# Two transformer blocks on one core: another order and other queues for the first transfers, and products of ones ahead of the work

## What is computed

```python
h = rmsnorm(x, norm_attn[l])
proj = h @ w_in[l]
qa, ka, va, qb, kb, vb = jnp.split(proj, splits, axis=-1)
...
yb = diff_attention(qb, kb, vb, lam)
yb = (rmsnorm(yb, subln[l], SUBLN_EPS) * (1.0 - lam_init)).astype(x.dtype).reshape(B, S, B_WIDTH)
x = x + jnp.concatenate([ya, yb], axis=-1) @ w_out[l]
h = rmsnorm(x, norm_ffn[l])
x = x + (jax.nn.silu(h @ w_gate[l]) * (h @ w_up[l])) @ w_down[l]
```

## Time and profile before

| | us |
|---|---|
| median of 3 runs | 2584.1 |
| lowest and highest | 2583.82, 2584.75 |
| the profiled execution | 2584.64 |
| its span | 2582.8 |
| TensorE busy in it | 2562.9 (99%) |
| VectorE, ScalarE, GpSimd busy | 1453.2, 1224.1, 104.4 |

### The profile page before, as it was taken

One profiled execution on the slowest core, in us unless ns is written; L12 is line 12 of the kernel. 1 busy time (PEld: TensorE's weight loads), 2 busy tenths in 40 slices (PEclk: granted clock), 3 DMA queues, 4 the chain that ended last, 5 costly groups with the idle time before them and its releaser, 6 DMA issues.

```text
span 2582.8 us, 40276 instructions
## 1 busy us (share of the span) xinstructions
PE 2562.9 (99%) x14246; PEld 2280.2 (88%) x14246; DVE 1453.2 (56%) x1743; ACT 1224.1 (47%) x1677; POOL 104.4 (4%) x171
## 2 busy tenths in 40 slices
PE   8999999999999999999999999999999999999999
PEld 8999988888888888888899888788999899998997
DVE  5555555555555555555455545465576646765674
ACT  5665545444344434455455544544454434543443
POOL 1111100000000000000000000100000000000000
PEclk9999999999999999999999999999999999999999
DMA  7555556665665566666555655555555555555554
GB/s 214 155 159 162 168 183 186 189 188 192 193 191 187 189 194 191 191 196 188 166 168 170 187 170 172 163 171 185 176 181 184 195 189 185 181 188 194 173 191 165
DMA packets 328631, 469.37 MB, mean 182 GB/s; under 512 B 21911, under 2 KB 137810, under 8 KB 328402
## 3 DMA queue, kind: packets, MB, share of 16 engines
q1 hardware_dynamic: 328530, 468.04, 58.1%
HBM read 465.87 MB, written 2.10 MB: 181 GB/s over the span
## 4 chain that ended last, share of the span: by engine, by line
PE 84%; issue 14%; POOL 1%; SPq 0%; DMA 0%; DVE 0%; ACT 0%; POOLq 0%; DVEq 0%; ACTq 0%
PE ps L429 20%; PE ps L431 20%; PE ps L430 20%; PE ps L443 7%; PE ps L442 7%; PE ps L441 7%; PE ps L498 1%; PE ps L645 1%; PE ps L676 0%; PE ps L549 0%; POOL head_rstd L1844 0%; PE ps L480 0%; PE ps L486 0%; PE ps L568 0%; SPq L328 0%
## 5 line engine op out<-in xcount | busy, mean ns | idle before, releaser
L1276 DVE TENSOR_TENSOR w_lo<-raw,w_hi 128x1024 fp32r<-128x1024 f32 (+1 forms) x928 | 1095.3, 1185 | 1080.3 <-ACT w_hi L879 1079.0
L879 ACT ACTIVATE w_hi<-raw 128x1024 fp32r<-128x1024 f32 (+1 forms) x928 | 947.7, 1025 | 1151.0 <-PE ps L431 961.6
L429 PE MATMUL ps<-w_hi,xT_hi 128*128 128x512 f32 (+1 forms) x2400 | 906.8, 378 | 2.9 <-DVE w_lo L1276 2.8
L431 PE MATMUL ps<-w_hi,xT_lo 128*128 128x512 f32 (+1 forms) x2400 | 893.6, 372 | 0.0
L430 PE MATMUL ps<-w_lo,xT_hi 128*128 128x512 f32 (+1 forms) x2400 | 892.9, 372 | 0.0
L429 PEld LDWEIGHTS ps<-w_hi,xT_hi 128*128 128x128 f32 x2400 | 451.5, 188 | 69.4 <-issue 6.6
L431 PEld LDWEIGHTS ps<-w_hi,xT_lo 128*128 128x128 f32 x2400 | 451.1, 188 | 64.3
L430 PEld LDWEIGHTS ps<-w_lo,xT_hi 128*128 128x128 f32 x2400 | 451.7, 188 | 62.4
L441 PE MATMUL ps<-yT_hi,w_hi 128*128 128x256 f32 x1408 | 398.6, 283 | 0.0
L443 PE MATMUL ps<-yT_hi,w_lo 128*128 128x256 f32 x1408 | 398.5, 283 | 0.0
L442 PE MATMUL ps<-yT_lo,w_hi 128*128 128x256 f32 x1408 | 398.5, 283 | 0.0
(11 more groups left out here) (191 smaller groups left out, 994.4 us busy)
## 6 DMA issues: line engine op xcount, KB each, us to landing
raw<-in_w_up SPq DMA_DIRECT2D x264, 512.0 KB, 3.6
raw<-in_w_down SPq DMA_DIRECT2D x176, 512.0 KB, 4.4
raw<-in_w_in SPq DMA_DIRECT2D x112, 512.0 KB, 3.7
raw<-in_w_in SPq DMA_DIRECT2D x256, 192.0 KB, 2.6
raw<-in_w_gate SPq DMA_DIRECT2D x88, 512.0 KB, 3.5
raw<-in_w_out SPq DMA_DIRECT2D x60, 512.0 KB, 4.1
raw<-in_w_in SPq DMA_DIRECT2D x64, 384.0 KB, 3.3
raw<-in_w_proj_m SPq DMA_DIRECT2D x16, 512.0 KB, 3.5
```

The source lines that it names most:

```text
L429: pe.matmul(o, hi[:, q], w_hi[n % NS][:, k, 0:width], start=first, stop=False)
L431: mm = pe.matmul(o, lo[:, q], w_hi[n % NS][:, k, 0:width], start=False, stop=last)
L879: nc.scalar.activation(w_hi[n % NS][:, :, 0:width], raw[n % NS][:, :, 0:width], ACT.Copy).then_inc(hi_ready, 1)
L1276: v.tensor_tensor(w_lo[n % NS][:, :, 0:width], raw[n % NS][:, :, 0:width], f32(w_hi[n % NS][:, :, 0:width]), ALU.subtract).then_inc(lo_rea ...
```

## The change

- SP asks for x first, and in eight pieces of 256 columns (256 KB), one ahead of unit 0 and one behind each of units 0 to 6. Piece j counts `x_landed[j % 4]`; pieces 4 to 7 are asked for only when piece j - 4 has landed. TensorE waits for piece 0 and 1 each ahead of its pair, and for each later pair's own.
- The identity and then the gain rows are asked for by ScalarE, as the first thing it does.
- The other 21 small transfers are asked for by GpSimd, between its memsets and `factor(1, rstd)`: fourteen (`small`) when `lo_ready` has reached `NS + 1`, that is behind split 0, and seven (`late`: `rope_a`, `tri`, `causal`, `ln_count`, gate biases) when it has reached `NS + 10`, behind split 9. The late ones count `late_landed`, for which VectorE waits ahead of phase `in_a` and GpSimd ahead of the rope steps of `in_a`.
- TensorE multiplies `ones` by `ones` nine times (`N_WARM`) into a bank that unit 0 overwrites, as soon as `ones` is set and before it waits for the gain rows.
- `small_T` and `parameters` move from behind unit 8 to behind unit 9, and ScalarE's Exp of lambda from 9 to 10.

```diff
-            sp.dma_start(gain_rows[0:KT, 0, :], a["norm_attn"][0].rearrange("(k c) -> k c", c=P)).then_inc(rows_landed, 16)
-            sp.dma_start(ident[:], a["c_ident"]).then_inc(ident_landed, 16)
...
             def load_x(j):
-                cols = slice(j * W, (j + 1) * W)
-                sp.dma_start(x[:, :, cols], x_in[:, :, cols]).then_inc(x_landed[j], 16)
+
+                cols = slice(j * 2 * P, (j + 1) * 2 * P)
+                if j >= 4:
+                    sp.wait_ge(x_landed[j % 4], 16 * (j // 4))
+                sp.dma_start(x[:, :, cols], x_in[:, :, cols]).then_inc(x_landed[j % 4], 16)
...
-            heads_turn("in_b", 0, C3, load_small)
+            heads_turn("in_b", 0, C3, lambda u: load_x(u + 1) if u < 7 else None)
...
             def start_more(j):
-                pe.wait_ge(x_landed[j // 2], 16)
+                pe.wait_ge(x_landed[j % 4], 16 * (j // 4 + 1))
...
+            pe.wait_ge(const_set, 1)
+            for j in range(N_WARM):
+                pe.matmul(ps[1][:, 0:P], ones[:], ones[:], start=True, stop=True)
             pe.wait_ge(rows_landed, 16)
             pe.wait_ge(ident_landed, 16)
             pe.transpose(ps[0][:, 0:KT], gain_rows[0:KT, 0, :], ident[0:KT, 0:KT]).then_inc(rows_T, 1)
-            pe.wait_ge(x_landed[0], 16)
             for j in range(2):
+                pe.wait_ge(x_landed[j], 16)
                 start_T(j)
...
-                if u == 8:
+                if u == 9:
                     small_T()
...
+            act.dma_start(ident[:], a["c_ident"]).then_inc(ident_landed, 16)
+            act.dma_start(gain_rows[0:KT, 0, :], a["norm_attn"][0].rearrange("(k c) -> k c", c=P)).then_inc(rows_landed, 16)
             act.wait_ge(const_set, N_CONST)
...
-                if u == 9:
+                if u == 10:
                     act.wait_ge(lam_step, 2)
...
-                if u == 8:
+                if u == 9:
                     parameters()
...
+            pool.wait_ge(lo_ready, NS + 1)
+            for dst, src in small:
+                pool.dma_start(dst, src).then_inc(small_landed, 16)
+            pool.wait_ge(lo_ready, NS + 10)
+            for dst, src in late:
+                pool.dma_start(dst, src).then_inc(late_landed, 16)
             pool.wait_ge(const_set, N_CONST)
```

More of the change, by code:

```diff
@@ L104 @@
 N_CONST = 5 + NS
-N_SMALL = 21
-X_BEHIND = (0, 2, 3)
+N_SMALL, N_LATE = 14, 7
+N_WARM = 9
 START_BANKS = (4, 5, 6, 7, 2, 3, 4, 5)
@@ L252, in two_blocks @@
         rows_landed, ident_landed = sem("rows_landed"), sem("ident_landed")
-        small_landed, gate_w_landed, final_landed = sem("small_landed"), sem("gate_w_landed"), sem("final_landed")
+        small_landed, late_landed, gate_w_landed, final_landed = sem("small_landed"), sem("late_landed"), sem("gate_w_landed"), sem("final_landed")
         const_set = sem("const_set")
@@ L1400, in _ @@
                 turn("in_b", i, 16, behind, WH)
+            dve.wait_ge(late_landed, 16 * N_LATE)
             def behind(u):
@@ L1811, in _ @@
                 pool.sem_inc(s, FREE)
+            small = [(gain_rows[j * KT:(j + 1) * KT, 1, :], (a[name] if name == "norm_final" else a[name][0]).rearrange("(k c) -> k c", c=P))
+                     for j, name in enumerate(("norm_ffn", "norm_final", "norm1_g_2", "norm2_g_2"))]
+            c0 = G_SUBLN - G_FFN
+            small += [(gain_rows[c0:c0 + 1, 1, :], a["subln"]), (gain_rows[c0 + 1:c0 + 2, 1, :], a["q_norm_g_2"]),
+                     (gain_rows[c0 + 2:c0 + 3, 1, :], a["k_norm_g_2"]),
+                     (gain_rows[c0 + 3:c0 + 3 + 2 * M_HEADS, 1, :], a["m_norm_g_2"][0].rearrange("h (e c) -> (h e) c", c=P)),
+                     (rope_b[:], a["c_rope_b"]), (lam_in, a["lambda_qk"][0].partition_broadcast(P))]
+            small += [(conv_rows[:, j, :], a["conv_w_2"][0, j].rearrange("(k c) -> k c", c=P)) for j in range(3)]
+            small += [(conv_rows[:, 3, :], a["conv_b_2"][0].rearrange("(k c) -> k c", c=P))]
+            late = [(rope_a[:], a["c_rope_a"]), (tri[:], a["c_tri"]), (causal[:], a["c_causal"]),
+                    (ln_count[:], a["c_count"].rearrange("p t s -> p (t s)")),
+                    (gate_bias[:, 0:HEADS], a["fox_f_bias_2"][0].partition_broadcast(P)),
+                    (gate_bias[:, HEADS:HEADS + M_HEADS], a["m_i_bias_2"][0].partition_broadcast(P)),
+                    (gate_bias[:, HEADS + M_HEADS:NG], a["m_f_bias_2"][0].partition_broadcast(P))]
+            assert len(small) == N_SMALL and len(late) == N_LATE
+            pool.wait_ge(lo_ready, NS + 1)
[4 more added lines that the diff above has]
+                pool.dma_start(dst, src).then_inc(late_landed, 16)
             pool.wait_ge(const_set, N_CONST)
@@ L1852, in _ @@
             pool.wait_ge(hb.qk_T, FREE + HEADS)
+            pool.wait_ge(late_landed, 16 * N_LATE)
             with pool.Fori(0, 8) as i:
```

## The result

The changed kernel takes 2591.12 us (median of nine runs, 2589.62 to 2592.08) where the kernel before takes 2584.57 (nine runs, 2583.82 to 2585.40): ratio 1.0026, 95% interval 1.0018 to 1.0034. That is 6.55 us slower, against a forecast of 6.8. The spans of the two profiled executions differ by 7.0.

The account below looks back on a forecast made before the run. TensorE, busy 2562.9 of 2582.8 us, was taken as the bound. The first head 4.5 us later despite a start 3.5 sooner, plus 2.3 for the fallen clock, made +6.8 on the 2584.1 median: 2590.9, range 2581.4 to 2596.0.

Parts of the forecast that it names:

- The stall: Seven GpSimd issues and split 9's wait delay rstd to 39.6; first head's transposes at 45.1, 4.5 us later than before.
- G: Start of the kernel: TensorE reaches unit 2 sooner by 3.5 us, 1.2 from the chain and 2.3 from the clock.
- c: Price of one DMA issue on GpSimd, taken as 0.9 us between 0.43 and 1.78.
- 2 us are safe: Ahead of unit 0: TensorE's clock survives 2 us of idleness, since 3.7 us passed before the only fall seen.
- Rival 3: At the start: the ones don't raise the clock, G is 1.2, all behind it 2.3 later; 2593.2 us, chance 0.10.
- From split 11 to the head: ScalarE's split 11 to the first head's transposes: 5.05 us as before, plus 0.4 for the parameters.
- The move of the parameters: VectorE's copies of the parameters, one unit later behind split 13, delay the first head's transposes by 0.4 us.
- The clock behind the stall: After 8.2 us of idleness TensorE restarts at half rate at the first head, costing 2.3 us, bounds 0 and 3.
- Rival 2: At the first head: the stall comes but the clock stays up; +4.5 us, 2588.6, chance 0.13.
- What was at nothing: At the start: identity and gain rows on ScalarE's queue cost nothing, landing before the ones end even if 1 us later.
- SP's relief: The 21 small transfers leave SP's queue, some 10 us of issuing, which gains nothing on the path.
- Rival 1: GpSimd's issues hardly hold it up, c near 0, deciding at 0.26; 1.8 of G left, 2582.3 us, chance 0.15.

Follow-up runs that it names:

- The ones in the gaps: The run with the parameters back plus six products of ones, in TensorE's two waits ahead of the first multiply: 2582.20 us, ratio 0.9992.
- the run with the parameters back: Changed kernel with late transfers behind split 4, and `small_T`, `parameters` and the Exp back at units 8, 8 and 9: 2582.32 us, ratio 0.9993.
- the ones in the stall: Changed kernel plus twenty products of ones behind unit 10, while TensorE waits for the first head: 2588.94 us, ratio 1.0017.

## Why the prediction was right, point by point

**The stall: right in place and cause.** The wait was to be ScalarE's for rstd behind seven issues of GpSimd, with TensorE's at the first head. Both are there, 5.45 and 6.00. rstd was put at 39.6 and came at 38.47 + 0.72 = 39.2; the head's transposes at 45.1, and they started at 45.03. Moving the set by one number took it away. The issues are 3.7 of it. The wait for split 9 ahead of them is a part of its own, as the prediction had it: before, the mean for rstd started 34.33 - 18.36 = 16.0 us behind unit 2, and the issues start 34.33 - 16.52 = 17.8 behind it. No run takes that wait away and leaves the issues.

**That 45.1 is hit so closely is luck: two terms are off and cancel.** The gain G was put at 3.5 and is 18.36 - 16.52 = 1.84. The issue was put at c = 0.9 and costs 0.53, so seven take 3.7 instead of 6.3. The start of the stall came 2.0 later than I had it (34.33 against 32.3), 1.7 of it by G; the seven issues were 2.6 shorter.

**G: the failed step is "2 us are safe".** The ones' end (5.1 for 5.0) and the first multiply (9.39 for 9.3) were right. The clock did rise early, at about 6.5. But it fell again at 9.9, after waits of 1.22 and 1.06 with four transposes between them, and nine of unit 0's twelve multiplies ran 0.32 apart. I had taken 3.7 us, from the one fall in the trace, as if a shorter wait couldn't do it; one case shows no threshold. The ones in the gaps show that these waits were the cause: the clock came up at 4.1 in that run as in the one without them, and there it fell at 7.5, at the end of a wait of 1.63, where with the gaps filled it stayed. The second piece of x landed at 7.7, not near 6.3, which made one of them. Rival 3, that the ones don't raise the clock, was wrong in its mechanism but nearer in its G than the forecast (1.2 against 1.84 measured, where the forecast had 3.5): they raised it, and it didn't last.

**c: a price without a row.** The range from 0.43 to 1.78 held it; I took 0.9 by GpSimd's arithmetic of 0.46 to 1.08, and passed over rows that cover 128 partitions too and take 0.19 and 0.20. It was near SP's issue instead, 0.1 above its 0.43. The Trainium skill's ratio ("DMA: Bandwidth & Descriptors", Latency and other measured facts), scaled, had given 0.7; the trace has 0.53. With the right c and the wrong G the forecast would have been 2588.3, with both right 2589.9. Three slips in the working change nothing: c = 0.7 gives 2589.5 and not 2589.4, c = 1.6 gives 2595.8 and not 2596.0, and TensorE's waits behind the first multiply are the three listed, not four.

**From split 11 to the head.** Put at 5.05 + 0.4 = 5.45, measured 39.23 to 45.03 = 5.80. Of the rope step, one small product (L1840) took 1.02 where its like took 0.3 in the chain before, with VectorE's subtractions of two SBUF operands (L1259, 41.77 to 43.85) beside it:

```profile
41.77 2.08 DVE L1259 TENSOR_TENSOR w_lo<-raw,w_hi 128x768 fp32r<-128x768 f32 x2 [0.71 <-ACT w_hi L860]
...
43.01 1.02 POOL L1840 TENSOR_TENSOR rot_v<-stage,rope_b 128x64 f32<-128x64 f32 x1
```

In the run with the parameters back it ran beside other work of VectorE and took 0.37. The Trainium skill ("SBUF — State Buffer", Who interferes with whom) says that a VectorE instruction with two SBUF inputs contends with GpSimd instructions that read SBUF; the traces agree: in the first 200 us of both kernels this product takes 1.02 to 1.04 in each head in which such a subtraction runs beside it for 0.85 us, and 0.32 to 0.37 in the others. No run here tries it alone. The move of the parameters was put at 0.4; under the stall it was hidden behind the rope step, and without the stall it costs 1.3. That term was too small by 0.9. With `small_T` behind unit 9 a wait of 0.30 has also come up at 34.18, which the run with the parameters back doesn't have.

**The clock behind the stall.** Put at 2.3, with bounds of 0 and 3, behind an idleness of 8.2 us that was 6.0. From the lengths in the chain it is 12.88 - 10.26 = 2.6, from the ones in the stall 2.2. Rival 2 is out: the clock does fall there.

**What was at nothing.** The identity and the gain rows on ScalarE's queue: without the ones the transpose of the gain rows waits until 4.74, where it started at 3.18 before, so they land 1.6 later and not 1. The ones cover that in the changed kernel; in the run with the parameters back, where the clock rose at 4.1 and the ones ended sooner, 0.34 of waiting showed. SP's relief is nothing, as put. The gap at unit 8 came again with its 0.44 (31.56 in the changed kernel), and that at unit 2 with 0.23.

**Rival 1** (issues that hardly hold GpSimd up, 2582.3) is out: they took 0.53 each, and it decides at 0.26. That the run with the late set early and the parameters back also has 2582.3 is no support for it: there the issues cost as much and stand where nobody waits behind them, and G is 3.0 in its profile, not 3.5.

The best versions tried (2582.2 to 2582.3) are 2.1 to 2.2 us below the kernel before by medians, and each interval still reaches 1.0001 or 1.0002, so none is shown to be faster.

## What to carry to other kernels

Work that is moved to an idle engine's queue goes in front of whatever that engine does next: look up the next instruction there, who waits for it, and its slack, before anything else. Here rstd had 0.3 us of slack on an engine that is 4% busy. A wait and seven issues of 0.53 ahead of it held ScalarE up for 5.45 us and TensorE for 6.0, and with the clock that fell they cost 7.1 to 7.3 us. Filling one wait with products of ones bought nothing here while other waits followed before the real work, and even a first unit at full clock was lost again further on.

## What wasn't expected of the hardware

A DMA issue on GpSimd took 0.48 to 0.58 each for 1 row or 128 (0.76 for the first), hardly more than the 0.43 on SP. TensorE's clock fell to half after waits of 1.22 and 1.06 us that followed one another, in the run with the parameters back at the end of a single one of 1.63, and in another run stayed full through one of 2.38 that followed 25 us at full clock. How short or how placed a wait has to be for the clock to survive these runs don't settle, and the time at which it rose under the same ones differed from run to run, from 4.1 to 6.5 us, and in one it didn't rise until 14.0.
